# One decoder layer on one core: the first LayerNorm of blocks 1 to 3 normalises first and multiplies by its gain later, and the table of matmul rows is made by cost

## The reference, cut to what matters

```python
mix = token_mixer(x, ...)      # z = x @ w_in; recurrence and short convolution; gates; @ w_branch_a / b; @ w_out
x = layer_norm(ALPHA * x + mix, ln1_g, ln1_b)
x = layer_norm(ALPHA * x + peer(x, pk_w_q, sub_keys, u, v), ln2_g, ln2_b)
x = x + sigmoid(x @ ple_w_gate) * (p @ ple_w_proj)
# layer_norm: (x - mean) * rsqrt(var + eps) * g + b
# peer, per token: 8 heads, queries (x @ w_q), scores against 128 + 128 sub-keys, the 16 best of the
# 256 sums, then sum over the 8*16 chosen experts e of softmax weight * gelu(u[e] . x) * v[e]
```

## Time and profile before

| | |
|---|---|
| time, median of 3 runs | 1788.03 us (1782.82 to 1788.03) |
| the profiled execution: own time, span | 1787.28 us, 1785.3 us |
| PE busy | 1572.3 us, 88% of the span |
| DVE busy | 1322.0 us, 74% |
| ACT busy | 780.5 us, 44% |
| POOL busy | 497.0 us, 28% |
| moved by DMA | 654.35 MB, 367 GB/s over the span |

### The profile page before, as it was taken

One profiled execution on the slowest core, in us unless ns is written; L12 is line 12 of the kernel. 1 busy time (PEld: TensorE's weight loads), 2 busy tenths in 40 slices (PEclk: granted clock), 3 DMA queues, 4 the chain that ended last, 5 costly groups with the idle time before them and its releaser, 6 DMA issues. The chain is left out here.

```text
span 1785.3 us, 16920 instructions
## 1 busy us (share of the span) xinstructions
PE 1572.3 (88%) x5008; PEld 876.8 (49%) x5008; DVE 1322.0 (74%) x2717; ACT 780.5 (44%) x1936; POOL 497.0 (28%) x528
## 2 busy tenths in 40 slices
PE   9999999999999978999888668888889879788778
PEld 7888888766555546454344222333333323232224
DVE  4454588699988999578877876876666677766676
ACT  6666695422222124354343434434444443444453
POOL 0000000122332222323333433433333333333341
PEclk9999999999999988999899989999999999999999
DMA  5113289999999999999999999999999999999994
GB/s 210 66 67 141 98 323 397 353 417 409 415 416 416 416 395 356 411 377 413 402 422 410 417 421 422 421 420 422 421 421 422 421 415 422 421 421 419 421 422 180
DMA packets 104501, 654.35 MB, mean 367 GB/s; under 512 B 10336, under 2 KB 25440, under 8 KB 28128
## 3 DMA queue, kind: packets, MB, share of 16 engines
q0 software_dynamic: 73728, 536.90, 72.9%
q1 hardware_dynamic: 30400, 115.92, 17.0%
q10 hardware_dynamic: 288, 0.52, 0.1%
HBM read 651.21 MB, written 2.10 MB: 366 GB/s over the span
## 5 line engine op out<-in xcount | busy, mean ns | idle before, releaser
L2122 PE MATMUL psum<-uv,diag 128*128 128x512 f32 x1400 | 699.8, 631 | 184.2 <-ACT diag L997 180.7
L1607 DVE CUSTOM_DVE_ANT_0 uv<-uv,psum 128x1024 f32<-128x1024 f32 x512 | 623.0, 1217 | 298.3 <-DMA uv<-in_pk_uv,idx 291.8
L726 POOL DMA_INDIRECT uv<-in_pk_uv,idx x512 | 494.6, 966 | 1253.3 <-PE psum L2122 560.3
L2122 PEld LDWEIGHTS psum<-uv,diag 128*128 128x128 f32 x1400 | 254.8, 196 | 600.5 <-ACT diag L997 380.4
L985 ACT ACTIVATE gelu<-dots 128x1 f32<-128x1 f32 x512 | 103.5, 202 | 755.5 <-DVE dots L1607 753.2
L1620 DVE SCALAR_TENSOR_TENSOR oT<-uv,coef,oT 128x1024 f32<-128x1024 f32 x157 | 201.0, 1281 | 1.5 <-ACT coef L989 1.5
L989 ACT ACTIVATE coef<-gelu,weight 128x1 f32<-128x1 f32 x512 | 150.9, 295 | 16.6
L997 ACT ACTIVATE diag<-ident,coef 128x128 f32<-128x128 f32 x350 | 140.6, 402 | 11.5
L2022 PE MATMUL psum<-xT,raw 128*128 128x384 f32 x384 | 125.8, 486 | 0.0
L1858 PE MATMUL psum<-xTh,w_hi 128*128 128x512 f32 x248 | 98.6, 398 | 0.0
L1858 PE MATMUL psum<-xTl,w_hi 128*128 128x512 f32 x248 | 96.8, 390 | 0.0
(11 more groups left out here) (295 smaller groups left out, 1856.6 us busy)
## 6 DMA issues: line engine op xcount, KB each, us to landing
raw<-in_w_in SPq DMA_DIRECT2D x24, 1024.0 KB, 8.7
raw_a<-in_w_a SPq DMA_DIRECT2D x12, 1024.0 KB, 4.7
raw<-in_pk_w_q SPq DMA_DIRECT2D x10, 1024.0 KB, 9.1
raw_y<-in_w_in SPq DMA_DIRECT2D x8, 1024.0 KB, 6.8
uv<-in_pk_uv,idx POOLq DMA_INDIRECT x512, 14.7
raw<-in_w_branch_a SPq DMA_DIRECT2D x6, 1024.0 KB, 7.2
raw_w<-in_pk_w_q SPq DMA_DIRECT2D x6, 1024.0 KB, 9.1
raw<-in_w_out SPq DMA_DIRECT2D x5, 1024.0 KB, 14.9
```

The costliest lines, as they stand in the source:

```text
L726: pool.indirect_dma_start(row_uv(r)[:], None, pk_uv, bass.IndirectOffsetOnAxis(idx[:, i % 2, j:j + 1], 0)).then_inc(row_loaded(r)[0], 16)
L1607: V.tensor_tensor_reduce(u, u, x_cur[:], 1.0, 0.0, ALU.mult, ALU.add, dots[:, r % 32:r % 32 + 1]).then_inc(dot_done, 1)
L2122: last = T.matmul(B[i][:], diag[:, n % DR, :], row_uv(r)[:, D + i * 512:D + (i + 1) * 512], start=(r in FIRST), stop=last_of_block, skip_g ...
```

## The change

Five edits:
1. The unit table. Instead of an even spread over rows 0 to 62, a unit's matmul goes to the first row at which the cost so far, 0.654 a matmul and 4.3 for each query job already met, is no more than an even share. The last rows of units 2 to 23 move 1 to 3 rows later, those of units 24 to 34 mostly by 1 or 2, and the last ones stay.
2. The first LayerNorm of blocks 1 to 3. `norm1_scale` and `norm1_shift` go. Now the statistics are aggregated in their own row, one row later `normed` computes (x - mean) * rstd in one instruction, and `gained` multiplies by the gain and adds the bias in two instructions at `GAINED_ROW` = 109, 113 and 117. The transpose takes the block as `normed` leaves it, and gain and bias are put on the transposed block by ScalarE: 8 activations of 128x128 for a block instead of 2 of 128x512.
3. The transposes come one row earlier (97, 101, 105), and with them the queries of heads 0 to 2 and their searches.
4. The merges of tiles 8 to 15 on VectorE come 1 row after their matmuls' row instead of 3.
5. `x1_done`, for which the load of `w_gate` waits, is now signalled by `gained`: for block 3 at row 117, where it was at row 105.

```diff
@@ unit table and rows
-        UNIT_ROW += [[(UNIT_MM * n + i) * MERGE0 // (UNIT_MM * (len(UNITS) - EARLY)) for i in range(UNIT_MM)]
-                     for n in range(len(UNITS) - EARLY)]
+        UNIT_COST, QUERY_COST = 0.654, 4.3
+        MMS = UNIT_MM * (len(UNITS) - EARLY)
+        ROW_COST = (MMS * UNIT_COST + len(QUERY0_ROW) * QUERY_COST) / MERGE0
+
+        def unit_row(m):
+
+            for r in range(MERGE0):
+                asked = len([q for q in QUERY0_ROW.values() if q <= r])
+                if (m + 1) * UNIT_COST + asked * QUERY_COST <= ROW_COST * (r + 1):
+                    return r
+            return MERGE0 - 1
+
+        UNIT_ROW += [[unit_row(UNIT_MM * n + i) for i in range(UNIT_MM)] for n in range(len(UNITS) - EARLY)]
...
-        TURN_ROW = [None] + [NORM_ROW[b] + 3 for b in range(1, TB)]
+        TURN_ROW = [None] + [NORM_ROW[b] + 2 for b in range(1, TB)]
+        GAINED_ROW = [None] + [TURN_ROW[-1] + 4 * b for b in range(1, TB)]
@@ ScalarE, turn_out
-                    dst = oT[:, 4 * kh:4 * kh + 4, b * P:(b + 1) * P]
-                    nc.scalar.activation(dst, B[bank(r)][:].rearrange("p (k t) -> p k t", t=P), ACT.Copy).then_inc(t_act, 1)
+                    for k in range(4 * kh, 4 * kh + 4):
+                        step = nc.scalar.activation(oT[:, k, b * P:(b + 1) * P], B[bank(r)][:, k % 4 * P:k % 4 * P + P],
+                                                    ACT.Identity, bias=vecs[:, BIAS1 + k:BIAS1 + k + 1],
+                                                    scale=vecs[:, GAIN1 + k:GAIN1 + k + 1])
+                    step.then_inc(t_act, 1)
@@ ScalarE, tail_row
-                    if r == NORM_ROW[b] + 1:
+                    if r == NORM_ROW[b]:
                         root_of(b, ln_var, ln_root, True)
@@ VectorE
             def norm1_stats(b):
                 dve.wait_ge(*t_reader(USE["out", 1, 3, b]))
                 norm_stats(x_of(b), ln_step)
-
-            def norm1_scale(b):
-                norm_scale(b, tiled(x_of(b)), tiled(x_of(b)), ln1[0], ln_step, ln_var)
+                dve.wait_ge(ln_step, 2 * b + 3)
+                V.bn_aggr(mean_var[:], stats[:].rearrange("p a s -> p (a s)")).then_inc(ln_var, 1)
+
+            def normed(b):
+                norm_rstd(b, ln_root, ln_rec)
+                dve.wait_ge(ln_rec, b + 1)
+                V.tensor_scalar(x_of(b), x_of(b), mean_var[:, 0:1], rstd[:, 1:2],
+                                ALU.subtract, ALU.mult).then_inc(x1n_done, 1)
+
+            def gained(b):
+                x = tiled(x_of(b))
+                dve.wait_ge(t_done, USE["turn", 1, b, 1] + 1)
+                V.tensor_tensor(x, x, ln1[0], ALU.mult).then_inc(ln_step, 1)
+                dve.wait_ge(ln_step, 2 * (TB - 1) + 3 + b)
+                V.tensor_tensor(x, x, ln1[1], ALU.add).then_inc(x1_done, 1)
...
-                    if r == MERGE_ROW[KT * n + KT - 1] + 3:
+                    if r == MERGE_ROW[KT * n + KT - 1] + (3 if n < 8 else 1):
                         merge(1, n // 4, n % 4)
...
                     if r == NORM_ROW[b] + 1:
-                        norm1_scale(b)
-                    if r == NORM_ROW[b] + 2:
-                        norm1_shift(b)
+                        normed(b)
+                    if r == GAINED_ROW[b]:
+                        gained(b)
@@ TensorE, turn_x
-                    pe.wait_ge(x1_done, b + 1)
+                    pe.wait_ge(x1n_done, b + 2)
```

More of the change, by code:

```diff
@@ L1445, in gained0 @@
                 V.tensor_tensor(tiled(x0_sb[:]), tiled(x0_sb[:]), ln1[1], ALU.add).then_inc(x1_done, 1)
-            def norm1_shift(b):
-                norm_rstd(b, ln_root, ln_rec)
-                norm_shift(b, tiled(x_of(b)), ln1[1], ln_step, ln_rec, x1_done)
             LOWEST = float(np.finfo(np.float32).min)
```

## The result

| | before | after |
|---|---|---|
| time, median | 1784.13 us (1782.82 to 1788.03, 7 runs) | 1791.88 us (1790.68 to 1794.55, 7 runs) |
| ratio, 95% interval | | 1.0039 [1.0027, 1.0051] |
| the profiled execution: own time, span | 1787.28, 1785.3 us | 1791.88, 1789.9 us |
| PE, DVE, ACT, POOL busy | 1572.3, 1322.0, 780.5, 497.0 us | 1573.0, 1323.3, 782.8, 497.8 us |

The change makes the kernel 0.39% slower, by some 7 us. I had forecast 1785 us and a gain of 2.5 us: the time lies at the upper end of the range (which reached to 1792), and the sign is wrong. With more runs the median of before is 1784.1, not 1788.0, so the profiled execution of before is 3.2 us slower than a usual one.

A forecast was written before the change was run, and what follows sets the result against it. DMA was taken to bound 810 to 1750 us and VectorE most of 600 to 720. Savings of 5.4 and 1.1 us, less 4 for the later `w_gate`, gave -2.5 from about 1788: 1785 us, range 1778 to 1792.

The forecast's parts named there:

- Taken as 0, at most 1.5 us: ScalarE's 24 small copies replacing 6 large ones: 4.6 us more work, expected to cost 0, at most 1.5 us.
- it can follow: -6.5 us: Stretch to 716 us: VectorE ends 6.5 us sooner, and the DMA, idle 8.5 us there, turns all of it into time.
- LayerNorm, -5.4 us: VectorE before 716 us: one instruction replaces two passes for each of three blocks, 5.4 us less work.
- 701 to 703: Sign to look for: the time in us at which VectorE's dot of row 103 should come.
- Merges, -1.1 us: Earlier merges let TensorE start output tiles some 7 us sooner, removing VectorE's 1.1 us wait for them.
- Unit table, 0: Moving unit matmuls changes no work and neither bound: 0, between a gain of 2 us and a loss of 3.
- Gain and bias on VectorE, 0: Six passes, 7.4 us, at rows 109 to 117, hidden in VectorE's 20 free us: cost 0.
- The later `w_gate`, +4 us, bounds 0 to 8: Loading `w_gate` at row 117 leaves a DMA hole between 704 and 745 us; cost 4 us, bounds 0 and 8.
- scores at 738, row 117 at 742, issue at 745: Forecast times in us for the end of head 0's scores, the dot of row 117 and the start of `w_gate`.
- Rival 1: The DMA hole doesn't open and the 6.5 us are kept: 1781.5 us, or 1779.5 with all idle DMA used; chance 0.33.
- Rival 2: TensorE waits about 12 us at row 124 for head 2's queries if `w_gate` starts only at 752: 1793.5 us; chance 0.13.
- Rival 3: Nothing moves: the unit table holds TensorE up, or the hole equals the saving: 1788 us; chance 0.14.

The follow-up runs named there:

- e10: Kernel before, with ScalarE copying each transposed block in 8 small activations with scale and bias instead of 2; ratio 1.0004.
- e14: Whole change, with ScalarE's copies of transposed blocks 1 and 2 moved to rows 100 and 104, behind the roots; ratio to the kernel before 1.0019.
- e13: e9 with ScalarE's copies of transposed blocks 1 and 2 moved to rows 100 and 104, behind the roots; ratio to the kernel before 0.9998.
- e9: Kernel before with one-pass LayerNorm; transposes, copies and queries in their old rows, gain and bias at rows 107, 108 and 109; ratio 1.004.
- e15: e13 plus the earlier merges of tiles 8 to 15; ratio to the kernel before 0.9992.
- e16: e14 with gain and bias at rows 106, 107 and 108, so that `w_gate` loads earlier; ratio to the kernel before 1.0006.
- e1: Kernel before with the new unit table alone; ratio 1.0002.
- e2: Kernel before with the earlier merges of tiles 8 to 15 alone; ratio 0.9994.
- e11: Kernel before with only the load of `w_gate` held back until the dot of row 117; ratio 1.0019.
- e17: e13 with gain and bias at rows 109, 113 and 117, so that `w_gate` loads late; ratio to the kernel before 1.0006.
- e7: Whole change with gain and bias four rows later, at rows 113, 117 and 121, and `w_gate` behind them; ratio to the kernel before 1.0089.
- e12: Kernel before with the queries of heads 0 to 2, their scores and searches one row earlier; ratio 1.0017.
- e5: Whole change with ScalarE's copies of all three transposed blocks one row later; ratio to the kernel before 1.0036.
- e8: Kernel before with the LayerNorm edits (2, 3, 5), ScalarE's copies one row later, gain and bias at rows 106 to 108; ratio 1.0034.

## Why the prediction was wrong

**Two steps failed.** The first is "Taken as 0, at most 1.5 us" for ScalarE. I priced the copies by their work, and the work was right (8.7 us for 24; e10: no cost). But I moved the copies one row earlier and the roots one row earlier without asking what is queued behind the copy on ScalarE, and how long TensorE keeps it waiting. That was to be read before the run: in before too ScalarE waits 5.2 us for a transpose in 600 to 720 us. Undoing this order and nothing else takes 0.20 of the 0.39% away (e14), and 0.42% in the old rows (e13 against e9).

The second is "it can follow: -6.5 us", by which VectorE's saved time was to become DMA time in full. In e15, which has the one-pass LayerNorm, the early merges and neither fault, it is 1.4 us, and not even that is sure. By medians of the ratios the way from there to the change is: -1.4 us (e15), +2.5 for the unit table and the transposes, queries and searches one row earlier (e16), +2.3 for the late `w_gate` (e14), +3.6 for ScalarE's order, together +7.0. Against the forecast of -2.5 the miss is 9.5 us: 5.1 of it is the saving that didn't come, 3.6 ScalarE's order, 2.5 the earlier rows, for which I had no term, less 1.7 for `w_gate`. Each of these steps is known to about 2 or 3 us either way, so which of the two failed steps weighs more is likely and not certain.

**LayerNorm, -5.4 us.** The saving on VectorE was there: with the roots ahead (e14) row 103 stands at 700.2 us, where e1 has it at 706.5, even a little ahead of the 701 to 703 that I had given for that dot; in the change it came at 705.2. The one instruction takes 862 ns, not 751, 0.3 us in all. What failed is the sentence that the DMA "can follow". With the merges, transposes and queries in the rows of before (e13), row 103 is 5.7 us sooner than in e1, row 128 is 3.5 sooner and row 248 1.9; the medians don't differ (0.9998, at best 0.11%). The idle time of the DMA before 710 us falls only from 9.0 us in e1 to 6.4 in e13, and the stretch 785 to 810 us takes part of that back (329 GB/s for 359). So I counted VectorE's time as DMA time, 1 to 1; e13's trace shows less than half, and its runs nothing that can be told from zero. The merges alone show the same: row 103 at 703.4 us, 3.1 sooner, for 1.1 us of time. Why not more is argued and not tested: rows are still read every 3.6 us up to row 103, against 2.5 for the DMA, so its buffers stay full, and the weight loads move with the rows.

**Merges, -1.1 us.** e2 measures 0.9994, which is 1.1 us less, with an interval from -2.7 to +0.5. TensorE's long wait did shrink as said; I had not seen that weights from the DMA would be next (4.4 us).

**Unit table, 0.** Right (e1).

**Gain and bias on VectorE, 0.** Their 7.4 us were hidden as far as the runs show: e16 has all six passes at rows 106 to 108 and e17 at rows 109 to 117, and neither is clear of before.

**The later `w_gate`, +4 us, bounds 0 to 8.** The mechanism is there. The hole in 730 to 760 us is 30 x (1 - 341/421) = 5.7 us. Adding the late load costs 0.19% in before (e11, 3.4 us), which is clear of noise. In the change itself its price is not clear: removing it pays 0.13% (e14 to e16, 2.3 us) and adding it to e13 costs 0.08% (e17, 1.4 us), both with intervals that overlap. The size was in the bounds; the time wasn't. I said scores at 738, row 117 at 742, issue at 745. It was 744.0, 750.1 and 755.07: the first hole took the 5 us, and ScalarE, which takes rows in order, sat 6.5 and 6.8 us at query tiles of head 0. The clock did not stay up either: TensorE's granted clock is 0.50 in 709 to 712 us in both traces.

**The rivals.** Rival 1 is out, since the hole opened. Rival 2's mechanism did not occur in the change (no wait of TensorE for `raw<-in_pk_w_q`) though `w_gate` came three us later than the 752 that I gave as its condition; with four rows more it does, 10.3 us (e7), near the 12 that I had worked out. Rival 3, that nothing moves, is what the parts come to once both ScalarE's order and the load are mended (e16, 1.0006); with the order alone 1.0019 is left.

**The base.** 1788 was the highest of three runs and their median at once, with 5 us between them. Against 1784.1 the forecast of -2.5 us would have been 1781.6, a miss of 10 us. By idle time of the DMA against e1, the stage up to 710 us brought +1.6 (10.6 for 9.0) where I had -6.5; 710 to 760 us +5.2 (6.4 for 1.2) where I had +4; and the rest +0.4 (4.1 for 3.7). So by these traces 8 of the 10 us are the first stage, in which both failed steps lie.

What stays open: how much of the last 0.06% in e16 is the early queries, which cost 0.17% alone (e12), and where in the trace e12 loses it; and how much of a sooner row 103 can be turned into time at all. In e5 and e8 the root of block 2 still stood behind the copy of block 1 (both in row 99), and VectorE waited 4.0 us for roots in 600 to 720 us in each. That this is why they stayed at 1.0036 and 1.0034 fits e14, where the copy comes a row later than in e5, but for e8 no run tests it.

## What to carry to other kernels

When an instruction is moved on an in-order engine, list what stands behind it in that queue and who waits for that, and read in the old trace how long the engine already waits at this instruction: an idle wait that cost nothing becomes a stall once something urgent stands behind it. Time taken off one engine is worth only the idle time of the resource that bounds the whole, so add that idle time up stretch by stretch; here the span was 1769 us plus it in all nineteen traces, give or take 1.6 us. Even that idle time is a ceiling and not a promise: 5.7 us less on VectorE's side brought nothing measurable here (e13). And a load that seems to be free because it fills slack is worth its place: moved later, it leaves a hole in one stage and competes in the next.

## What the runs showed of the hardware

ScalarE's switches between gelu and root take 1.28 us each, and no more: the load starts 0.02 us after the coefficient's end (695.53 + 0.29, then 695.84), and the root follows 0.02 us after the load. The Trainium skill's page "ScalarE: Activation LUTs" (What ACT_TABLE_LOAD costs) gives 1283 ns for the load, and the trace agrees, but also some 1380 ns for a drain at each switch, of which the rows show nothing; here the measurement decides.

GpSimd's issues of gathers did not become clearly slower beside the new VectorE instruction. The row of after:

```profile
L738 POOL DMA_INDIRECT uv<-in_pk_uv,idx x512: 932/936/1867, 336.6 to 1754.8; - x171
```

The median is that of the earlier trace rows and the longest is below it. Two issues overlap an instruction of `normed`: one took 0.94 us (at 677.88), the other 1.15 (at 697.48), but one at 687.96 us with no `normed` beside it took 1.14. The Trainium skill's page "SBUF — State Buffer" (Who interferes with whom) has VectorE in a two-port mode shut GpSimd out; the three instructions of `normed` show no price for it above these 0.2 us.
